# A two-layer trunk on one core: the head mean squares of layer 1 split into rounded halves and summed one head unit later

## The reference

```python
def rms_norm(x, gain):
    xf = x.astype(jnp.float32)
    y = xf * lax.rsqrt(jnp.mean(xf * xf, axis=-1, keepdims=True) + NORM_EPS)
    return (y * gain.astype(jnp.float32)).astype(x.dtype)

# differential_attention, 8 heads of 128 output columns
p = jax.nn.softmax(sc, axis=-1)
a = p[:, :, 0] - lam * p[:, :, 1]
return jnp.einsum('bhqk,bkhe->bqhe', a.astype(v.dtype), v)
...
o = rms_norm(o, subln) * (1.0 - lambda_init)
return o.reshape(b, s, B_HEADS * 2 * HEAD_DIM) @ w_out
```

## Time and profile before

| | us |
|---|---|
| median of 3 runs | 1174.99 |
| lowest and highest of the 3 | 1174.76, 1175.63 |
| the profiled execution's own time | 1174.54 |
| its span, first to last instruction | 1172.8 |
| mean granted TensorE clock, share of full | 0.994 |
| PE busy, weight loads (PEld) busy | 1140.1, 966.2 |
| DVE busy, ACT busy | 688.9, 462.2 |

### The profile page before, as it was taken

How to read it: one execution, slowest core, us unless ns; L and a number is a source line. 1 busy time by engine, 2 the same in 40 slices (tenths; PEclk the granted TensorE clock), 3 DMA queues, 4 the chain that set the end, 5 groups by cost and what they waited for, 6 DMA issues and landing times.

```text
span 1172.8 us, 15982 instructions
## 1 busy us (share of the span) xinstructions
PE 1140.1 (97%) x5752; PEld 966.2 (82%) x5752; DVE 688.9 (59%) x1153; ACT 462.2 (39%) x939; POOL 19.0 (2%) x36
## 2 busy tenths in 40 slices
PE   7999899999999999998999999999999999999997
PEld 6998688888888878887999988778888888888886
DVE  5588765565565553337577777855556556553334
ACT  6577653122122222336455556554212212222324
POOL 4100000000000000000000000000000000000000
PEclk8999999999999999999999999999999999999999
DMA  7211223323323222325112311214332332213222
GB/s 225 72 37 37 73 88 92 96 84 107 105 74 107 72 72 94 102 89 162 55 54 69 94 36 36 72 40 122 108 92 86 107 103 76 89 54 105 92 91 106
DMA packets 146603, 101.94 MB, mean 87 GB/s; under 512 B 12073, under 2 KB 139270, under 8 KB 146566
## 3 DMA queue, kind: packets, MB, share of 16 engines
q1 hardware_dynamic: 146566, 101.45, 28.1%
HBM read 99.34 MB, written 2.10 MB: 86 GB/s over the span
## 4 chain that ended last, share of the span: by engine, by line
PE 87%; DVE 7%; ACT 4%; issue 1%; DMA 1%; SPq 0%; DVEq 0%; ACTq 0%
PE ps L529 22%; PE ps L531 22%; PE ps L530 21%; PE ps L594 15%; PE ps L608 2%; PE ps L746 2%; ACT prob L1091 1%; DVE w_lo L1354 1%; DVE h_lo L1383 1%; PE ps L772 1%; PE ps L818 1%; DVE ot_lo L1563 1%; ACT w_hi L1014 1%; ACT prob L1101 1%; DVE den L1441 0%
## 5 line engine op out<-in xcount | busy, mean ns | idle before, releaser
L1014 ACT ACTIVATE w_hi<-raw 128x512 fp32r<-128x512 f32 (+2 forms) x212 | 192.5, 940 | 302.6 <-PE ps L531 299.7
L529 PE MATMUL ps<-h_hi,w_lo 128*128 128x512 f32 x704 | 274.7, 390 | 0.0
L531 PE MATMUL ps<-h_hi,w_hi 128*128 128x512 f32 x704 | 273.9, 389 | 0.0
L530 PE MATMUL ps<-h_lo,w_hi 128*128 128x512 f32 x704 | 273.9, 389 | 0.0
L1354 DVE TENSOR_TENSOR w_lo<-raw,w_hi 128x512 fp32r<-128x512 f32 (+2 forms) x204 | 215.6, 1082 | 6.2 <-ACT w_hi L1014 6.2
L530 PEld LDWEIGHTS ps<-h_lo,w_hi 128*128 128x128 f32 x704 | 132.1, 188 | 27.9 <-issue 0.5
L529 PEld LDWEIGHTS ps<-h_hi,w_lo 128*128 128x128 f32 x704 | 132.1, 188 | 27.7 <-issue 0.5
L531 PEld LDWEIGHTS ps<-h_hi,w_hi 128*128 128x128 f32 x704 | 132.1, 188 | 27.6
L594 PE MATMUL ps<-w_hi,h_lo 128*128 128x384 f32 x384 | 133.4, 347 | 8.6 <-DVE w_lo L1354 4.5
L594 PE MATMUL ps<-w_hi,h_hi 128*128 128x384 f32 x384 | 133.2, 347 | 0.0
L594 PE MATMUL ps<-w_lo,h_hi 128*128 128x384 f32 x384 | 132.5, 345 | 0.0
(11 more groups left out here) (188 smaller groups left out, 1583.2 us busy)
## 6 DMA issues: line engine op xcount, KB each, us to landing
raw<-in_ffn_w_up SPq DMA_DIRECT2D x88, 512.0 KB, 4.5
raw<-in_ffn_w_down SPq DMA_DIRECT2D x44, 512.0 KB, 3.3
raw<-in_b_w_in SPq DMA_DIRECT2D x24, 512.0 KB, 4.9
raw<-in_a_w_out SPq DMA_DIRECT2D x4, 1024.0 KB, 4.9
raw<-in_b_w_out SPq DMA_DIRECT2D x4, 1024.0 KB, 4.7
raw<-in_a_w_in SPq DMA_DIRECT2D x3, 1024.0 KB, 5.8
x_tok<-in_x SPq DMA_DIRECT2D x4, 512.0 KB, 4.8
out<-x_tok SPq DMA_DIRECT2D x8, 256.0 KB, 2.0
```

Source lines behind the costliest of these rows:

```text
L529: pe.matmul(out_, a_lo, b_hi, start=start, stop=False)
L530: pe.matmul(out_, a_hi, b_lo, start=False, stop=False)
L531: return pe.matmul(out_, a_hi, b_hi, start=False, stop=stop)
L1014: act.activation(w_hi[:, s, at], raw[:, s, at], ACT.Copy).then_inc(hi_done, 1)
```

## The change

The mean square of head u - 1 is taken out of the end of unit u - 1 and put into unit u, for u = 1 to 7; the one of head 7 stays at the end of unit 7 in float32. ACT copies the squares, rounded to float32r, into `osq_hi` (a slice of `qt_hi` that layer 1 doesn't use), DVE makes the rest `osq_lo`, and PE sums both with two float32r matmuls after `scores_b(u, 2)`. On ACT, `exps_b(u, 1)`, `take` and `weights(0)` now come ahead of `rsqrt_head(u - 1)` and `high_out_b(u - 1)`. On DVE, `combine_b(u, 1)`, `low_v` and `weights(0)` now come ahead of `norm_head(u - 1)`, which stands ahead of `maxima_b(u, 2)`; `low_out_b(u - 1)` follows that. `ones_d` is declared float32r and read as float32 where it was before; this costs nothing by itself.

```diff
-        ones_d = sb("ones_d", [P, P])
+        ones_d = sb("ones_d", [P, P], F32R)
...
+        osq_hi, osq_lo = qt_hi[:, 2, :], qt_lo[:, 2, :]
...
+            def head_mean_square(u):
+
+
+                pe.wait_ge(osqlo_done, u + 1)
+                pe.matmul(ps[:, TB, :], ones_d[:, :], osq_lo, start=True, stop=False)
+                pe.matmul(ps[:, TB, :], ones_d[:, :], osq_hi, start=False, stop=True).then_inc(oms_done, 1)
...
                 scores_b(u, 2)
+                if not (isinstance(u, int) and u == 0):
+                    head_mean_square(u - 1)
                 run(slabs, n[1])
...
-                pe.wait_ge(osq_done, u + 1)
-                pe.matmul(ps[:, TB, :], ones_d[:, :], osq[:, :], start=True, stop=True)\
-                  .then_inc(oms_done, 1)
+                if not more:
+                    pe.wait_ge(osq_done, u + 1)
+                    pe.matmul(ps[:, TB, :], ones_d[:, :].bitcast(F32), osq[:, :], start=True, stop=True)\
+                      .then_inc(oms_done, 1)
                 run(slabs, 24)
...
                 high_p("B", u, 0)
                 if before:
+                    act.wait_ge(osq_done, u)
+                    act.activation(osq_hi, sq[:, 0, :], ACT.Copy).then_inc(osqhi_done, 1)
+                exps_b(u, 1)
+                if more:
+                    take("B", u + 1, 1 - s, 1)
+                weights(0)
+                if before:
                     rsqrt_head(u - 1)
-                exps_b(u, 1)
-                if more:
-                    take("B", u + 1, 1 - s, 1)
-                if before:
                     high_out_b(u - 1)
-                weights(0)
                 weights(1)
                 high_p("B", u, 1)
...
                 low_p("B", u, 0)
                 if before:
+                    dve.wait_ge(osqhi_done, u)
+                    dve.tensor_tensor(osq_lo, sq[:, 0, :], osq_hi.bitcast(F32), ALU.subtract)\
+                       .then_inc(osqlo_done, 1)
+                combine_b(u, 1)
+                if more:
+                    low_v("B", u + 1, 1 - s, 1)
+                weights(0)
+                if before:
                     norm_head(u - 1)
-                combine_b(u, 1)
-                if more:
-                    low_v("B", u + 1, 1 - s, 1)
+                maxima_b(u, 2)
                 if before:
                     low_out_b(u - 1)
-                weights(0)
-                maxima_b(u, 2)
                 low_p("B", u, 1)
```

More of the change, by code:

```diff
@@ L251, in trunk @@
         osq_done = sem("osq_done")
+        osqhi_done = sem("osqhi_done")
+        osqlo_done = sem("osqlo_done")
         oms_done = sem("oms_done")
@@ L497, in _ @@
                 pool.memset(invf[:, i:i + 1], inv_freq(i)).then_inc(const_done, 1)
-            pool.memset(ones_d[:, :], 1.0 / D).then_inc(const_done, 1)
+            pool.memset(ones_d[:, :].bitcast(F32), 1.0 / D).then_inc(const_done, 1)
             pool.memset(eps[:, :], EPS).then_inc(const_done, 1)
@@ L559, in mean_square @@
                 pe.wait_ge(ss_done, KC * norm)
-                pe.matmul(ps[:, TB, :], ones_d[:, :], ssacc[:, :], start=True, stop=True)\
+                pe.matmul(ps[:, TB, :], ones_d[:, :].bitcast(F32), ssacc[:, :], start=True, stop=True)\
                   .then_inc(ms_done, 1)
@@ L566, in mean_square_tok @@
                 for t in range(NT):
-                    ins = pe.matmul(ps[:, OBK, t:t + 1], ssacc[:, t * P:(t + 1) * P], ones_d[:, 0:1],
+                    ins = pe.matmul(ps[:, OBK, t:t + 1], ssacc[:, t * P:(t + 1) * P],
+                                    ones_d[:, 0:1].bitcast(F32),
                                     start=True, stop=True)
@@ L1283, in unit_b @@
                 if before:
-                    rsqrt_head(u - 1)
+                    act.wait_ge(osq_done, u)
+                    act.activation(osq_hi, sq[:, 0, :], ACT.Copy).then_inc(osqhi_done, 1)
                 exps_b(u, 1)
@@ L1287, in unit_b @@
                     take("B", u + 1, 1 - s, 1)
+                weights(0)
                 if before:
+                    rsqrt_head(u - 1)
                     high_out_b(u - 1)
-                weights(0)
                 weights(1)
@@ L1727, in unit_b @@
                 if before:
-                    norm_head(u - 1)
+                    dve.wait_ge(osqhi_done, u)
+                    dve.tensor_tensor(osq_lo, sq[:, 0, :], osq_hi.bitcast(F32), ALU.subtract)\
+                       .then_inc(osqlo_done, 1)
                 combine_b(u, 1)
@@ L1731, in unit_b @@
                     low_v("B", u + 1, 1 - s, 1)
+                weights(0)
+                if before:
+                    norm_head(u - 1)
+                maxima_b(u, 2)
                 if before:
                     low_out_b(u - 1)
-                weights(0)
-                maxima_b(u, 2)
                 low_p("B", u, 1)
```

## The result

The changed kernel took 1183.41 us in the median of 4 runs (1181.71 to 1184.58), against 1175.05 before: ratio 1.0067, 95% interval 1.0053 to 1.0081, or +8.4 us where +2.45 was forecast. Its profiled execution took 1182.64 us, with a span of 1180.9; the one before had 1174.54 and 1172.8. So the two profiles are 8.1 apart, and this is what they have to explain.

The account below looks back on a forecast made before the run. Middle units were taken as bound by PE tied with the ACT and DVE chain, unit 7 by the chain alone. 0.2 - 0.18 + 2.43 = +2.45 us on 1174.99 gave 1177.44 us, range 1175.4 to 1178.6.

Parts of the forecast that it names:

- The tie in a middle unit: Middle units: PE reaches `fill_qk` just as the ACT and DVE chain through `rope` does (0.35 start gap, 0.17 pace).
- PE's part: Seven units: float32 matmul of 0.86 us removed, float32r pair of 0.47 added, so PE work falls 0.39 us each.
- With everything ahead of the removed matmul unmoved: Unit 3: the first sum matmul starts at 655.49 - 0.86 = 654.63, in place of the slab matmul after the scores.
- The chain of the late norm: Units 1 to 5: ACT reaches `high_p(1)` 0.04 us late behind the moved norm, PE's 0.39 given back; +0.2 us altogether.
- Rival C: Hand-overs dearer throughout: 5 x 0.15 + 3.0 - 0.1 = +3.65 us, 1178.6; chance 0.12.
- Unit 6: Smaller weight pieces let ACT reach `high_p(1)` 0.18 us sooner: -0.18 us, bounds -0.39 and 0.
- Unit 7: Output chunk 6 waits for head 6's low half, starting at 760.55, not 758.12: +2.43 us, bounds +1.2 and +3.0.
- rival D: Clock falls behind unit 7's 2.3 us gap; the following 3.3 us take up to twice that, up to 1180.7; chance 0.03.
- B: Unit 7 costs half, as chunk 6's low half is ready sooner and the other branch rules: 1176.2 us; chance 0.12.
- E: Both gains, no cost: saving comes through and unit 7's chunk 6 doesn't wait, 7 x -0.39 = -2.7, 1172.3 us; chance 0.03.
- A: Saving comes through in units 1 to 5: -1.95 us in place of +0.2, total 1175.3, not slower; chance 0.12.

Follow-up runs that it names:

- late_f32: Changed kernel's order, but the mean square by the float32 matmul in the new place, without rounded halves, copy and subtraction: 1186.74 us, 1.0093 of the kernel before.
- sum_early: Changed kernel with the sum of the halves ahead of `scores_b(u, 2)`, nothing else: 1178.89 us, 1.0033 of the kernel before.
- best1: Changed kernel with take and tile 0's low half ahead of square and maximum, sum ahead of `scores_b(u, 2)`, head 6 as before: 1174.21 us, 0.9986 of before.
- take_first: Changed kernel with ACT's take ahead of the square and DVE's low half of tile 0 ahead of tile 1's maximum: 1178.87 us, 1.0031 of before.
- one_rounded: Kernel before, order kept, squares of heads 0 to 6 rounded and summed by one float32r matmul, low half left out: 1173.57 us, 0.9982 of before.
- before_take: Kernel before with only take moved ahead of the square and tile 0's low half ahead of tile 1's maximum: 1176.72 us, 1.0009 of before.
- gap_filled: only_head6 plus eight float32r matmuls with unused result in unit 7, between `probs_b(7, 1)` and output chunk 6: 1178.47 us, 1.0024 of before.
- only_head6: Heads 0 to 5 as in the kernel before, head 6 alone as in the changed kernel: 1180.13 us, 1.0031 of before.
- chunk6_late: Changed kernel with unit 7's output chunk 6 worked behind `probs_b(7, 2)`, not ahead of `values_b(7, 0)`: 1179.90 us, 1.0043 of before.

## Why the prediction was wrong, step by step

**The tie in a middle unit: right.** It said that the chain through `rope` is level with PE, so that PE's 0.39 us would be given back if ACT became late. late_f32, sum_early and best1 show both halves of that.

**PE's part: right in size.** The pair's matmuls start 0.34 apart, and the next slab 0.23 to 0.24 behind the second, as taken. When nothing else holds the unit, 0.32 to 0.36 us come through (best1).

**"With everything ahead of the removed matmul unmoved": this step failed.** I moved `probs_b(u, 0)` and the slabs behind it 0.86 us forward and asked only whether the scores would find their operand. The slab itself has a wait, for the bank that `low_v` gives back, and its end stood in the trace of before: 651.33, against a slab at 651.73. That leaves 0.35 us of room for a shift of 0.86, so 0.5 us of waiting. The prediction costed the removal of the matmul by its length, and never named it as the cover of something else. The size is shown three times: 0.49 us a unit in take_first, 0.33 in place of 0.63 in one_rounded, and in the profile after itself (0.51 to 0.54 from `probs_b` to the slab).

**The chain of the late norm: right mechanism, slightly short.** Forecast +0.04 a unit without the wait. take_first, where the wait is gone and the late norm stays, shows +0.05 in unit 1 (613.98 - 588.39 = 25.59 against 25.54) and +0.15 to +0.33 in the loop's units 2 to 5. (The exchange that it also has costs 0.08 to 0.17 a unit in before_take, but there through the float32 matmul, which take_first doesn't have in this place.) In these units, as the profile after shows for unit 3, the step from `norm_head` to `high_out_b` takes 0.13 (`norm_head` ends at 659.21 + 0.75 = 659.96, and ACT starts at 660.09) and not the 0.03 that I took. Rival C had allowed 0.15. Of the +0.33, which is unit 3's, 0.18 lie ahead of `probs_b(3, 0)`, and the changed kernel has them too (11.85 us from `fill_qk`, before 11.66): a slab there starts at 644.00 in the profile after, when DVE's low half of the weights is over (643.00 + 0.95). Why it is late in this unit alone stays open.

**Unit 6: -0.18 forecast, +0.37 found.** The same wait; without it, in take_first, it was -0.15.

**Unit 7: +2.43 forecast.** Without the fall of the clock it is +2.51 (take_first, gap_filled). The steps up to chunk 6 are within about 0.1 us of their places. In the profile after the clock fell and made it 3.86; that was rival D, to which I gave 0.03 and left out of the range. It should have had a large part: three of five profiles with such a gap show the lower clock behind it (after, only_head6 and late_f32, not take_first and chunk6_late). D's price, up to 3.3 us, was too high: it was 1.4. I had also misread the trace when I wrote that it shows a fall at the start only. The trace before has one between the two layers, behind 4.48 us of idle time, with a granted clock of 0.50 from 546 to 548 us:

```profile
544.97 0.45 PE L594 MATMUL ps<-w_hi,h_lo 128*128 128x384 f32 x1 [4.48 <-DVE w_lo L1354]
...
547.13 0.52 PE L594 MATMUL ps<-w_lo,h_hi 128*128 128x384 f32 x1
```

The sum of units, 3.35 - 0.2 = 3.15, unit 6, 0.55, the clock, 1.4, and the start of this execution, 0.5, make 5.6 of the 5.65 us between forecast and profile. Rivals B and E did not occur, and C was right on the dearer hand-over in the loop but not in unit 7. A was wrong as it stood, but best1 is what it described, once both causes are away.

## What to carry to other kernels

Whoever removes work from a full engine has to look at every wait of what moves forward, the buffer releases too, and not only at the operands: a step that took time was also cover, and its room is the distance from the releasing instruction's end to the start of what needs it. And when a result is moved later, follow it to the last consumer in every unit, the last one above all: where the pipeline runs out there is no other work to hide behind, and an order that is harmless in the middle costs its whole latency.

Before moving, price both places of a step: here the cheaper sum was worth 0.32 to 0.36 us a unit, and 0.9 us of place, with the wait for a bank, decided whether any of it was seen.

## What the runs showed of the hardware

Idle time of TensorE of only 2.4 us, with dense work on both sides, was followed by 1.2 GHz in three kernels' profiles (after, only_head6 and late_f32; in only_head6 a pace of 0.43 us between 512-column float32r matmuls, against 0.23) and by no loss in two (take_first with 2.38 us, chunk6_late with 2.62). Filled with unneeded matmuls it cost no clock in the one profile of that. I had taken the 1.33 us gap of before, which cost none, as the better guide; one_rounded shows a fall behind 1.11 and 0.38 us, once in thirteen profiles. The Trainium skill (TensorE: Matmul & The Clock Gate, HAM oscillation) warns of waits between bursts of matmuls, but of longer ones than these. The 4.48 us of before agree with it; the three falls behind 2.4 us show that a shorter wait is not safe.

A 128x128 by 128x512 float32 matmul held TensorE for 0.86 us before. A pair of float32r matmuls of the same size took 0.34 + 0.23 = 0.57 behind a group of scores in the changed kernel.
